# First mixer's last item spread over finer steps with full-row head weights and ScalarE copies; second mixer multiplies values and turns weights ahead of new scores

## Chip, cores and metric

One NeuronCore of one Trainium2 chip runs the whole program. The metric is the device time of one execution in microseconds (us), as the median of several runs. The program computes in float32; matmuls read float32r operands.

## What is computed

The input x is 512 tokens by 1024 features. Two blocks of two layers each follow one another. The change touches only the two attention mixers of the first block:

```python
def dilated_mixer(h, w_in, w_out):              # first mixer
    proj = (h @ w_in).reshape(B, S, 3 groups, 3, 16 heads, 64)
    for g, (window, dil) in enumerate(((128, 1), (512, 4), (2048, 16))):
        q, k = partial_rotary(proj[g, 0]), partial_rotary(proj[g, 1])
        o, lse = dilated_band_attention(q, k, proj[g, 2], dil, window // dil)
    wts = softmax(stack(lses), axis=groups)     # one weight per group, token, head
    o = einsum('gbsh,gbshd->bshd', wts, stack(outs))
    return o.reshape(B, S, 1024) @ w_out

def forgetting_mixer(h, w_in, b_f, w_out):      # second mixer
    q, k, v = h @ w_in;  c = cumsum(log_sigmoid(gates))
    s = q @ k^T / 8 + c_query - c_key, causal   # blocks of 128 queries
    return (softmax(s) @ v) @ w_out
```

After each mixer comes a SwiGLU layer, then a recurrent mixer and a retention mixer; these are unchanged.

## The kernel before

Activations lie feature by token. Every weight matrix is streamed in 353 units of 128 by 1024 through a ring of five slots. For each unit ScalarE rounds the weights into a high part WH (`split`, L1121) and VectorE computes the low part WL (L1711). TensorE multiplies in three passes, high by high, high by low and low by high, each a matmul with 512 columns. Instructions of each engine run in the order in which they are written; the order between engines is kept by semaphores.

The first mixer runs as six bodies (half of the heads by dilation group), each with 24 steps of 12 matmuls (L596 to L598 for queries and keys, L621 to L623 for values). Attention of the body before is strewn into the steps by a table written by hand: `place(phase, ticks, first, last)` spreads entries over the steps of a phase, phase 6 being the output projection (`AO`). An entry is one piece of attention for one item (a pair of heads): `scores` (L668, then mask and maximum on VectorE L1831, exponentials on ScalarE L1150), `turned` (the weights of head 0 or 1 transposed on TensorE L678 into bank 6, copied to A_PT by VectorE L1850 for head 0 and by ScalarE L1161 for head 1), `values` (L692, copied out to A_O by VectorE L1859), `weights` and `turn` (softmax over the three groups and its transposition, L701 and L707), `merge` (TensorE spreads one group's weights over the features of a tile, L715 and L716; VectorE multiplies A_O by it, L1883; GpSimd adds the groups, L1603 and L1607) and `low` (the high and low parts of the merged tile, L1171 and L1817). All engines walk through the same table.

The merge matmuls take 8 rows as operands: the weights of group g lie in rows 32g to 32g+7 of A_WH and A_WL, and A_SR holds a selection pattern in the same rows. Successive merges alternate between two banks of PSUM.

The output projection first works on feature tiles 0 to 3, four units of `pair_unit` with a step after every second of four row blocks (L596 to L598), then on tiles 4 to 7, four units with two steps each (L757 to L759), which read the A_YH and A_YL that `low` makes. R is the residual; VectorE adds the partial sums to it (L1939) after each of the first four units.

The second mixer has 88 steps of six matmuls and 32 items (a pair of heads by a block of 128 queries, so that an item has one to four blocks of keys). `forget_ticks` lists for item i the entries `norm` of i-1 (VectorE reciprocal L2047, GpSimd multiplication L1661), `scores` of i (L916; VectorE mask and maximum L2057 and L2059; ScalarE exponentials L1301), `values` of i-3 (L937; for the last block of a pair ScalarE makes B_OH, L1313, and VectorE B_OL, L2079) and `turned` of i-2, head 0; the next tick holds `turned` of head 1 (L926; copies L2076 on VectorE and L1309 on ScalarE). Both heads' transposes go to the same bank, so that those of head 1 wait for the copy of head 0. `place_b` gives each tick a step of its own, two or three steps per item, and two per item from step 66. These lines carry the order inside a step:

```python
                    (("norm", i - 1), 1 <= i <= B_ITEMS), (("scores", i), i < B_ITEMS),
...
                    (("values", i - 3), 3 <= i), (("turned", i - 2, 0), 2 <= i < B_ITEMS + 2)) if there])
...
                for entry in B_SPOT.get(g, ()):
                    forget(entry)
```

## Time and profile before

| | us |
|---|---|
| median of 3 runs | 2300.19 (2296.62 to 2302.95) |
| profiled execution, device time | 2301.07 |
| its span in the profile | 2299.3 |
| TensorE busy | 2227.8 |
| VectorE, ScalarE, GpSimd busy | 1203.8, 816.6, 492.5 |
| mean granted TensorE clock | 0.989 of full |

The span is that of the profiler; the execution's own time lies 1.8 us above it. A busy TensorE that is granted half its clock counts as busy, so the idle time and the clock are read apart. Matmuls of 512 columns last 0.39 us each and overlap, so that their spacing, not their length, is their cost.

### The profile page before, as it was taken

The page shows a single profiled execution, that of the slowest core. Times are in us where ns is not written, and L with a number is a line of the kernel's source. Part 1 is how long each engine was busy: PE and PEld are TensorE (multiplying, and loading weights), DVE is VectorE, ACT ScalarE, POOL GpSimd, SP SyncE. Part 2 cuts the span into 40 slices and gives each one's busy share as a digit, 9 for nine tenths or more (in the row PEclk, how much of TensorE's full clock was granted, in tenths as well). Part 3 has the DMA queues.
Part 4 walks back from the last instruction along what each step waited for, and adds up shares of the span by engine and source line. Part 5 has one row for each costly group of instructions (what it writes and reads, how often), then busy time and mean ns, then how long its engine had stood idle before and what let it go on. Part 6 is the DMA issues. An engine that isn't in the chain of part 4 may idle for free.

```text
span 2299.3 us, 26729 instructions
## 1 busy us (share of the span) xinstructions
PE 2227.8 (97%) x10598; PEld 1789.7 (78%) x10598; DVE 1203.8 (52%) x1995; ACT 816.6 (36%) x1360; POOL 492.5 (21%) x335
## 2 busy tenths in 40 slices
PE   8999999998999999999999999999998979999999
PEld 7788886887788888876667888888776857877877
DVE  4656556465654443355457444433788675443443
ACT  4434332434232222233433332322478323323322
POOL 2533234150511011123234110112111141100100
PEclk9999999999899999999999999999999999999999
DMA  4222221222233333332212333333332322222322
GB/s 154 83 65 83 74 83 56 65 77 62 67 98 94 99 98 95 101 102 74 92 56 83 93 100 95 98 101 93 92 94 81 100 69 83 87 78 75 96 71 85
DMA packets 85931, 198.27 MB, mean 86 GB/s; under 512 B 7328, under 2 KB 46496, under 8 KB 85808
## 3 DMA queue, kind: packets, MB, share of 16 engines
q1 hardware_dynamic: 83184, 189.62, 27.1%
q10 hardware_dynamic: 2624, 6.93, 0.9%
q8 instruction: 86, 1.41, 0.2%
q14 instruction: 37, 0.30, 0.1%
HBM read 194.40 MB, written 2.13 MB: 85 GB/s over the span
## 4 chain that ended last, share of the span: by engine, by line
PE 89%; DVE 5%; issue 2%; ACT 2%; POOL 1%; DMA 1%; SPq 0%; DVEq 0%; ACTq 0%; POOLq 0%
PE PS L550 52%; PE PS L596 6%; PE PS L598 5%; PE PS L597 5%; PE PS L621 2%; PE PS L623 2%; PE PS L622 2%; PE PS L1073 2%; PE PS L668 1%; PE PS L678 1%; PE PS L692 1%; PE PS L926 1%; PE PS L916 1%; PE PS L937 1%; PE PS L837 1%
## 5 line engine op out<-in xcount | busy, mean ns | idle before, releaser
L1711 DVE TENSOR_TENSOR WL<-WR,WH 128x1024 fp32r<-128x1024 f32 x353 | 468.2, 1332 | 732.8 <-ACT WH L1121 732.3
L1121 ACT ACTIVATE WH<-WR 128x1024 fp32r<-128x1024 f32 x353 | 371.1, 1056 | 692.0 <-DMA WR<-in_ws 680.9
L550 PE MATMUL PS<-XH,WH 128*128 128x512 f32 x1024 | 404.1, 395 | 18.9 <-ACT XH L1130 12.1
L550 PE MATMUL PS<-XL,WH 128*128 128x512 f32 x1024 | 400.5, 391 | 0.0
L550 PE MATMUL PS<-XH,WL 128*128 128x512 f32 x1024 | 400.5, 391 | 0.0
L550 PEld LDWEIGHTS PS<-XH,WH 128*128 128x128 f32 x1024 | 193.6, 189 | 63.4 <-issue 13.9
L550 PEld LDWEIGHTS PS<-XL,WH 128*128 128x128 f32 x1024 | 193.6, 189 | 41.4 <-issue 1.4
L550 PEld LDWEIGHTS PS<-XH,WL 128*128 128x128 f32 x1024 | 193.5, 189 | 40.5
L596 PE MATMUL PS<-XH,WH 128*128 128x512 f32 x544 | 224.8, 413 | 0.0
L598 PE MATMUL PS<-XH,WL 128*128 128x512 f32 x544 | 214.9, 395 | 0.0
L597 PE MATMUL PS<-XL,WH 128*128 128x512 f32 x544 | 214.3, 394 | 0.0
L1637 POOL TENSOR_TENSOR F_U<-F_G,F_U 128x1024 f32<-128x1024 f32 x22 | 52.6, 2392 | 399.5 <-DVE F_G L1977 399.5
L1615 POOL TENSOR_TENSOR A_SH<-A_SH,A_SIN 128x512 f32<-128x512 f32 x48 | 82.4, 1718 | 257.7 <-DVE A_SH L1897 257.7
L550 PE MATMUL PS<-HH,WH 128*128 128x512 f32 x352 | 136.9, 389 | 0.0
L550 PE MATMUL PS<-HL,WH 128*128 128x512 f32 x352 | 136.9, 389 | 0.0
L550 PE MATMUL PS<-HH,WL 128*128 128x512 f32 x352 | 136.9, 389 | 0.0
L1150 ACT ACTIVATE A_P<-A_P,A_ST 128x128 f32<-128x128 f32 (+1 forms) x192 | 79.7, 417 | 132.0 <-DVE A_ST L1840 132.0
L598 PEld LDWEIGHTS PS<-XH,WL 128*128 128x128 f32 x544 | 103.5, 190 | 23.4
L596 PEld LDWEIGHTS PS<-XH,WH 128*128 128x128 f32 x544 | 104.3, 192 | 21.9 <-issue 3.0
L597 PEld LDWEIGHTS PS<-XL,WH 128*128 128x128 f32 x544 | 104.2, 192 | 19.0
L550 PE MATMUL PS<-WH,XH 128*128 128x512 f32 x256 | 99.7, 389 | 0.0
L550 PE MATMUL PS<-WH,XL 128*128 128x512 f32 x256 | 99.6, 389 | 0.0
(327 smaller groups left out, 3715.9 us busy)
## 6 DMA issues: line engine op xcount, KB each, us to landing
WR<-in_ws SPq DMA_DIRECT2D x281, 512.0 KB, 3.6
WR<-in_ws SPq DMA_DIRECT2D x144, 256.0 KB, 3.2
B_CB<-gates ACTq DMA_DIRECT2D x8, 512.0 KB, 4.5
XTOK<-in_x SPq DMA_DIRECT2D x4, 512.0 KB, 5.9
out<-OUT SPq DMA_DIRECT2D x8, 256.0 KB, 2.0
R_D<-in_decay ACTq DMA_DIRECT2D x4, 256.0 KB, 2.6
GAIN<-in_post ACTq DMA_DIRECT2D x1, 512.0 KB, 4.8
CST<-in_cst SPq DMA_DIRECT2D x1, 256.0 KB, 6.5
```

The costliest lines, as they stand in the source:

```text
L550: mm = pe.matmul(PS[:, bank + o, :], l, r, start=first and kk == 0 and i == 0, stop=last and kk == 1 and i == 2)
L596: pe.matmul(PS[:, bank + o, :], WH[:, s, cols], hi[:, k, :], start=first, stop=False)
L597: pe.matmul(PS[:, bank + o, :], WH[:, s, cols], lo[:, k, :], start=False, stop=False)
L598: return pe.matmul(PS[:, bank + o, :], WL[:, s, cols], hi[:, k, :], start=False, stop=last)
L621: pe.matmul(PS[:, o, :], xh, wh, start=first and kk == 0, stop=False)
L622: pe.matmul(PS[:, o, :], xh, wl, start=False, stop=False)
L623: mm = pe.matmul(PS[:, o, :], xl, wh, start=False, stop=last and kk == 1)
L1121: nc.scalar.activation(WH[:, s, :], WR[:, s, :], ACT.Copy).then_inc(hi_ready, 1)
L1150: x = nc.scalar.activation(A_P[:, n % 2, h, w], A_P[:, n % 2, h, w], ACT.Exp, bias=stat(m, 0, 2 * pair + h, qb), accum_out=stat(m, 1, 2 * ...
L1615: nc.gpsimd.tensor_tensor(A_SH[:, r % 2, :], A_SH[:, r % 2, :], A_SIN[:, :], ALU.mult).then_inc(rot_m, 1)
L1637: nc.gpsimd.tensor_tensor(F_U[:, :, :], F_G[:, :, :], F_U[:, :, :], ALU.mult).then_inc(ht_ready, 1)
L1711: tt(WL[:, s, :], WR[:, s, :], WH[:, s, :].bitcast(F32), ALU.subtract).then_inc(lo_ready, 1)
```

## The change

1. **Output projection in finer steps.** In the first four units a step follows each row block (six matmuls): phase 6 has 24 steps instead of 16, numbers 0 to 15 of six matmuls and 16 to 23 of twelve.
2. **Last item table.** The entries of body 5 are placed by hand. The third item's scores come at step 22 of body 5 instead of step 0 of the projection; values come first in their steps; one or two merges stand in each of steps 8 to 14, the four `low` entries in steps 11, 13, 15 and 17.
3. **Copies.** Values of body 5 are copied to A_O by ScalarE instead of VectorE.
4. **Merges of the second half over 128 rows.** A new tile A_SEL (three patterns of 128 rows, made by three ScalarE copies at step 5 of the projection) takes the place of A_SR; A_WG, A_WH and A_WL become 128 rows, with zeros where no weights are. A_SEL lies over A_COS, A_SIN and A_SH.
5. **Second mixer.** Within a step the entries now stand as norm, values, turned, scores. VectorE sorts them as norm, turned, scores, values; ScalarE puts values first.

```diff
-        A_WG = a("A_WG", [P, TB, 96])
+        A_WG = a("A_WG", [P, TB, P])
...
-        late = scored(5)
...
-        place(5, late[:3], 18, 21)
-        place(6, late[3:], 0, 5)
-        place(6, [[("weights", 1)], [("turn", 1)]], 4, 5)
-        place(6, merged(1, (0, 1)) + [[("low", 0)]], 6, 7)
-        place(6, [[("low", 1)]] + merged(1, (2,)), 8, 8)
-        place(6, merged(1, (3,)) + [[("low", 2)]], 9, 9)
-        place(6, [[("low", 3)]], 10, 10)
+        place(5, [[last("scores", 0)], [last("scores", 1), last("turned", 0, 0)], [last("turned", 0, 1)]], 18, 21)
+        place(5, [[last("scores", 2)]], 22, 22)
+        place(6, [[last("values", 0), last("turned", 1, 0)], [last("turned", 1, 1), last("scores", 3)],
+                  [last("values", 1), last("turned", 2, 0)], [last("turned", 2, 1), ("weights", 1)],
+                  [last("values", 2), last("turned", 3, 0)], [last("turned", 3, 1)],
+                  [last("values", 3), ("turn", 1)], blended((0, 0), (0, 1)), blended((0, 2), (1, 0)),
+                  blended((1, 1), (1, 2)), blended((2, 0)) + [("low", 0)], blended((2, 1), (2, 2)),
+                  blended((3, 0)) + [("low", 1)], blended((3, 1), (3, 2)), [("low", 2)], [], [("low", 3)]], 1, 17)
...
-                    (("norm", i - 1), 1 <= i <= B_ITEMS), (("scores", i), i < B_ITEMS),
+                    (("norm", i - 1), 1 <= i <= B_ITEMS),
...
-                    (("values", i - 3), 3 <= i), (("turned", i - 2, 0), 2 <= i < B_ITEMS + 2)) if there])
+                    (("values", i - 3), 3 <= i), (("turned", i - 2, 0), 2 <= i < B_ITEMS + 2),
+                    (("scores", i), i < B_ITEMS)) if there])
...
+            return {"norm": 0, "turned": 1, "scores": 2, "values": 3}.get(entry[0], 4)
...
-                    pe.matmul(PS[:, bank, :], A_SR[rows, cols], A_WH[rows, :], start=True, stop=False)
-                    pe.matmul(PS[:, bank, :], A_SR[rows, cols], A_WL[rows, :], start=False, stop=True)\
+                    heads = A_SR[rows, cols] if half == 0 else A_SEL[:, g, cols]
+                    rows = slice(0, P) if half else rows
+                    pe.matmul(PS[:, bank, :], heads, A_WH[rows, :], start=True, stop=False)
+                    pe.matmul(PS[:, bank, :], heads, A_WL[rows, :], start=False, stop=True)\
...
+                elif ENTRIES[e][0] == "values" and ENTRIES[e][1] == 5:
...
+                    nc.scalar.activation(by_class(A_O[:, m % 4, pair, :], 2), classes_of(PS[:, O_BANK, :], 2), ACT.Copy)\
...
+                if i == 5:
+                    act.wait_ge(qk_ready, 48)
+                    for g in range(3):
+                        nc.scalar.activation(A_SEL[:, g, :].rearrange("p (h j) -> p h j", h=8),
...
-                for entry in B_SPOT.get(g, ()):
+                for entry in sorted(B_SPOT.get(g, ()), key=turned_first):
```

ScalarE at the passage from body 5 to the output projection, before (A_P and A_ST are the exponentials, A_V the copies of body 5's values out of PSUM):

```order
L1121 ACTIVATE WH<-WR 128x1024 [waits landed4]
L1230 ACTIVATE A_V<-PS,RB 128x512 [waits pv_done,rb_ready,v_half]
L1230 ACTIVATE A_V<-PS,RB 128x512
L1230 ACTIVATE A_V<-PS,RB 128x512 [waits unit_used]
L1230 ACTIVATE A_V<-PS,RB 128x512
L1121 ACTIVATE WH<-WR 128x1024 [waits landed0]
L1150 ACTIVATE A_P,A_ST<-A_P,A_ST 128x128 [waits nm_ready]
L1150 ACTIVATE A_P,A_ST<-A_P,A_ST 128x128 x3
L1150 ACTIVATE A_P,A_ST<-A_P,A_ST 128x128 [waits nm_ready]
L1150 ACTIVATE A_P,A_ST<-A_P,A_ST 128x128 x3
```

and now:

```order
L1138 ACTIVATE WH<-WR 128x1024 [waits landed4]
L1167 ACTIVATE A_P,A_ST<-A_P,A_ST 128x128 [waits nm_ready]
L1167 ACTIVATE A_P,A_ST<-A_P,A_ST 128x128 x3
L1167 ACTIVATE A_P,A_ST<-A_P,A_ST 128x128 [waits nm_ready]
L1167 ACTIVATE A_P,A_ST<-A_P,A_ST 128x128 x3
L1255 ACTIVATE A_V<-PS,RB 128x512 [waits pv_done,rb_ready,v_half]
L1255 ACTIVATE A_V<-PS,RB 128x512
L1255 ACTIVATE A_V<-PS,RB 128x512 [waits unit_used]
L1255 ACTIVATE A_V<-PS,RB 128x512
L1138 ACTIVATE WH<-WR 128x1024 [waits landed0]
L1185 ACTIVATE A_O<-PS 128x4x128 [waits y_sum,pv_done]
```

The exponentials of the third item have moved ahead of the four copies to A_V, and a copy to A_O stands ahead of the copy to A_PT.

TensorE at one item of the second mixer with three blocks of keys, before (B_K,B_Q are scores, B_PT,B_V values, CST,B_P transposes):

```order
L916 MATMUL PS<-B_K,B_Q 128x384 x2
L937 MATMUL PS<-B_PT,B_V 64x128 x8
L926 MATMUL PS<-CST,B_P 128x128
L596 MATMUL PS<-XH,WH 128x512
L597 MATMUL PS<-XL,WH 128x512
L598 MATMUL PS<-XH,WL 128x512
L596 MATMUL PS<-XH,WH 128x512
L597 MATMUL PS<-XL,WH 128x512
L598 MATMUL PS<-XH,WL 128x512
L926 MATMUL PS<-CST,B_P 128x128
```

and now:

```order
L954 MATMUL PS<-B_PT,B_V 64x128 x8
L943 MATMUL PS<-CST,B_P 128x128
L933 MATMUL PS<-B_K,B_Q 128x384 x2
L611 MATMUL PS<-XH,WH 128x512
L612 MATMUL PS<-XL,WH 128x512
L613 MATMUL PS<-XH,WL 128x512
L611 MATMUL PS<-XH,WH 128x512
L612 MATMUL PS<-XL,WH 128x512
L613 MATMUL PS<-XH,WL 128x512
L943 MATMUL PS<-CST,B_P 128x128
```

The scores have moved behind the values and the first transpose; the six matmuls of the step still lie between the two transposes.

VectorE at the same item, before (B_DG and B_CB are masks, B_OL the low part of a finished pair):

```order
L2057 ISA B_P,B_MX<-PS,B_CB 128x256
L2057 ISA B_MX 128x1
L2059 ISA B_P,B_MX<-PS,B_DG 128x128
L2059 ISA B_MX 128x1
L2068 TENSOR_SCALAR B_NM<-B_MX 128x1
L2057 ISA B_P,B_MX<-PS,B_CB 128x256
L2057 ISA B_MX 128x1
L2059 ISA B_P,B_MX<-PS,B_DG 128x128
L2059 ISA B_MX 128x1
L2068 TENSOR_SCALAR B_NM<-B_MX 128x1
L2079 TENSOR_TENSOR B_OL<-PS,B_OH 128x512
L2076 COPY B_PT<-PS 128x128
```

and now:

```order
L2078 RECIPROCAL B_RD<-B_DEN 128x2
L2107 COPY B_PT<-PS 128x128
L2088 ISA B_P,B_MX<-PS,B_CB 128x256
L2088 ISA B_MX 128x1
L2090 ISA B_P,B_MX<-PS,B_DG 128x128
L2090 ISA B_MX 128x1
L2099 TENSOR_SCALAR B_NM<-B_MX 128x1
L2088 ISA B_P,B_MX<-PS,B_CB 128x256
L2088 ISA B_MX 128x1
L2090 ISA B_P,B_MX<-PS,B_DG 128x128
L2090 ISA B_MX 128x1
L2099 TENSOR_SCALAR B_NM<-B_MX 128x1
```

The copy to B_PT, which was last, now comes ahead of masks and maxima, and B_OL follows them.

## Rows read from the trace of the kernel before

**Rows 1.** The page: busy us of each engine, share of the span, instructions.
```profile
PE 2227.8 (97%) x10598; PEld 1789.7 (78%) x10598; DVE 1203.8 (52%) x1995; ACT 816.6 (36%) x1360; POOL 492.5 (21%) x335
```

**Rows 2.** Windows: length, busy us of each engine, granted TensorE clock, DMA share, GB/s.
```profile
560.00:580.00 20.00, 16.28 (x58) 11.13 (x56) 12.20 (x16) 3.75 (x5) 5.35 (x4) 0.74 0.18 52
580.00:600.00 20.00, 16.54 (x60) 11.83 (x59) 8.98 (x10) 3.15 (x4) 5.37 (x4) 0.83 0.16 42
600.00:620.00 20.00, 20.00 (x90) 16.57 (x89) 17.21 (x18) 9.25 (x12) 14.74 (x11) 1.00 0.30 91
1015.00:1215.00 200.00, 187.30 (x1078) 131.62 (x1077) 101.62 (x395) 82.02 (x194) 62.96 (x79) 1.00 0.25 79
```

**Rows 3.** What TensorE waited for, 500 to 640 us: us, times, longest.
```profile
PE PS L757 <- DVE A_YL L1817: 4.7, 2, 2.8
PE PS L715 <- DVE A_O L1883: 2.5, 3, 0.9
PE PS L678 <- DVE A_PT L1850: 2.2, 1, 2.2
PE PS L701 <- issue: 0.9, 1, 0.9
```

**Rows 4.** TensorE timeline: start, length, line, operation, shapes, count, [idle before].
```profile
510.93 1.16 PE L668 MATMUL PS<-A_K,A_Q 64*128 64x128 f32 x16
...
563.38 0.50 PE L715 MATMUL PS<-A_WH,A_SR 8*128 8x512 f32 x2
563.72 0.40 PE L716 MATMUL PS<-A_WL,A_SR 8*128 8x512 f32 x2
...
574.34 0.77 PE L757 MATMUL PS<-A_YH,WH 128*128 128x512 f32 x1 [2.82 <-DVE A_YL L1817]
...
579.17 0.63 PE L759 MATMUL PS<-A_YH,WL 128*128 128x512 f32 x1
```

**Rows 5.** VectorE groups, 505 to 570 us: count, busy us, mean ns, idle before.
```profile
L1711 DVE TENSOR_TENSOR WL<-WR,WH 128x1024 fp32r<-128x1024 f32 x8 | 10.5, 1314 | 8.3 <-ACT WH L1121 8.3
L1859 DVE COPY A_O<-PS 128x512 f32<-128x512 f32 x4 | 4.3, 1068 | 3.0 <-PE PS L692 3.0
```

**Rows 6.** TensorE timeline: values of one item of the first mixer, transposes after them.
```profile
540.98 1.09 PE L692 MATMUL PS<-A_PT,A_V 128*64 128x128 f32 x16
542.01 0.66 PE L678 MATMUL PS<-CST,A_P 128*128 128x128 f32 x4
```

**Rows 7.** ScalarE timeline: exponentials of one item, copies of the values.
```profile
513.31 0.40 ACT L1150 ACTIVATE A_P<-A_P,A_ST 128x128 f32<-128x128 f32 x1 [6.80 <-DVE A_ST L1840]
...
516.32 0.19 ACT L1150 ACTIVATION_READ_ACCUMULATOR A_P<-A_P,A_ST 128x1 f32 x1
...
526.11 1.27 ACT L1230 ACTIVATE A_V<-PS,RB 128x512 f32<-128x512 f32 x2 [0.89 <-PE PS L623]
```

**Rows 8.** What TensorE waited for in the second mixer, 1015 to 1225 us.
```profile
PE PS L926 <- DVE B_PT L2076: 11.6, 12, 2.6
```

**Rows 9.** VectorE timeline around the longest of these waits.
```profile
1130.74 0.40 DVE L2057 CUSTOM_DVE_ANT_0 B_P<-PS,B_CB 128x256 f32<-128x256 f32 x1
...
1133.67 0.69 DVE L2079 TENSOR_TENSOR B_OL<-PS,B_OH 128x512 fp32r<-128x512 f32 x1 [1.26 <-ACT B_OH L1313]
1134.28 0.28 DVE L2076 COPY B_PT<-PS 128x128 f32<-128x128 f32 x1
```

**Rows 10.** TensorE timeline: scores of the item after it.
```profile
1136.34 1.13 PE L916 MATMUL PS<-B_K,B_Q 64*128 64x512 f32 x4
```

**Rows 11.** ScalarE timeline of that same item.
```profile
1139.51 0.73 ACT L1301 ACTIVATE B_P<-B_P,B_NM 128x512 f32<-128x512 f32 x1
...
1140.23 1.04 ACT L1121 ACTIVATE WH<-WR 128x1024 fp32r<-128x1024 f32 x1
```

**Rows 12.** A TensorE wait of 2.4 us elsewhere, and the window around its end.
```profile
1675.19 0.55 PE L1005 MATMUL PS<-CH,WH 128*128 128x512 f32 x1 [2.40 <-ACT L_R L1383]
...
1674.00:1678.00 4.00, 2.81 (x7) 2.27 (x8) 3.75 (x7) 3.99 (x7) 0.00 (x0) 0.69 0.09 36
```

More of the change, by code:

```diff
@@ L112, in program @@
         A_Y = a("A_Y", [P, 4, T])
+        A_SEL = sb("A_SEL", [P, 3, T], F32R, at=a.at)
         A_COS = a("A_COS", [P, T])
         A_SIN = a("A_SIN", [P, T])
+        A_SH = a("A_SH", [P, 2, T])
         A_P = a("A_P", [P, 2, 2, T])
         A_PT = a("A_PT", [P, 2, T])
-        A_SH = a("A_SH", [P, 2, T])
         A_MX = a("A_MX", [P, 2, 2, TB])
@@ L326, in program, with last, blended @@
         place(5, scored(4), 0, 14)
-        place(5, late[:3], 18, 21)
-        place(6, late[3:], 0, 5)
-        place(6, [[("weights", 1)], [("turn", 1)]], 4, 5)
-        place(6, merged(1, (0, 1)) + [[("low", 0)]], 6, 7)
-        place(6, [[("low", 1)]] + merged(1, (2,)), 8, 8)
-        place(6, merged(1, (3,)) + [[("low", 2)]], 9, 9)
-        place(6, [[("low", 3)]], 10, 10)
+        def last(kind, *rest):
+            return (kind, 5) + rest
+        def blended(*parts):
+            return [("merge", 1, t, j) for t, j in parts]
+        place(5, [[last("scores", 0)], [last("scores", 1), last("turned", 0, 0)], [last("turned", 0, 1)]], 18, 21)
[6 more added lines that the diff above has]
+                  blended((3, 0)) + [("low", 1)], blended((3, 1), (3, 2)), [("low", 2)], [], [("low", 3)]], 1, 17)
         for spot in sorted(SPOT):
@@ L411, in program, with turned_first, values_first @@
         place_b(forget_ticks(24, B_ITEMS + 3), 66, 86)
+        def turned_first(entry):
+            return {"norm": 0, "turned": 1, "scores": 2, "values": 3}.get(entry[0], 4)
+        def values_first(entry):
+            return 0 if entry[0] == "values" else 1
         B_TURNED = {7: [("q", 1, 0)], 8: [("q", 1, 1)], 15: [("k", 1, 0)], 16: [("k", 1, 1)],
@@ L735, in _ @@
                     pe.wait_ge(r_part, 2 * q - 2)
-                half_unit = pair_unit(U["AO"] + q, 0, XH, XL, 2 * (q % 2), True, True, x_ready(1))
-                for i in range(2):
+                half_unit = pair_unit(U["AO"] + q, 0, XH, XL, 2 * (q % 2), True, True, x_ready(1), every=1)
+                for i in range(4):
                     next(half_unit)
-                    for e in SPOT.get((6, 2 * q + i), ()):
+                    for e in SPOT.get((6, 4 * q + i), ()):
                         attend(e)
@@ L761, in _ @@
                             mm.then_inc(unit_used, 1)
-                    for e in SPOT.get((6, 8 + 2 * q + kk), ()):
+                    for e in SPOT.get((6, 16 + 2 * q + kk), ()):
                         attend(e)
@@ L1161, in attend @@
                     nc.scalar.activation(A_PT[:, 1, 0:w], PS[:, T_BANK, 0:w], ACT.Copy).then_inc(pt_copied, 1)
+                elif ENTRIES[e][0] == "values" and ENTRIES[e][1] == 5:
+                    _, m, i = ENTRIES[e]
+                    pair, segs, n = item(m, i)
+                    act.wait_ge(pv_done, n + 1)
+                    if pair == 0:
+                        act.wait_ge(y_sum, 8)
+                    nc.scalar.activation(by_class(A_O[:, m % 4, pair, :], 2), classes_of(PS[:, O_BANK, :], 2), ACT.Copy)\
+                        .then_inc(o_copied, 1)
                 elif ENTRIES[e][0] == "weights":
@@ L1232, in _ @@
             ao = U["AO"]
-            for i in range(16):
-                split(ao + i // 2 + 4)
+            for i in range(24):
+                split(ao + (i // 4 if i < 16 else i // 2 - 4) + 4)
+                if i == 5:
+                    act.wait_ge(qk_ready, 48)
+                    for g in range(3):
+                        nc.scalar.activation(A_SEL[:, g, :].rearrange("p (h j) -> p h j", h=8),
+                                             CST[:, IDENT + 32 * g:IDENT + 32 * g + 8].unsqueeze(2)
+                                             .to_broadcast([P, 8, HD]), ACT.Copy).then_inc(sel_ready, 1)
                 for e in SPOT.get((6, i), ()):
@@ L1318, in _ @@
                 split(bf + 9 + g // 4 + 4)
-                for entry in B_SPOT.get(g, ()):
+                for entry in sorted(B_SPOT.get(g, ()), key=values_first):
                     forget(entry)
@@ L1625, in _ @@
                         rotate(m, n)
-            for i in range(16):
+            for i in range(24):
                 for e in SPOT.get((6, i), ()):
@@ L1853, in attend @@
                     pair, segs, n = item(m, i)
-                    if closes(m, i):
+                    if closes(m, i) and m < 5:
                         g = A_BODIES[m][1]
@@ L1876, in attend @@
                     dve.wait_ge(st_hi, ENTRIES[e][1] + 1)
-                    tt(A_WL[0:96, :], PS[0:96, bank, :], A_WH[0:96, :].bitcast(F32), ALU.subtract)\
+                    tt(A_WL[:, :], PS[:, bank, :], A_WH[:, :].bitcast(F32), ALU.subtract)\
                         .then_inc(front_used, 1)
@@ L1930, in _ @@
             ao = U["AO"]
-            for i in range(16):
-                split(ao + i // 2 + 4)
+            for i in range(24):
+                split(ao + (i // 4 if i < 16 else i // 2 - 4) + 4)
                 for e in SPOT.get((6, i), ()):
                     attend(e)
-                if i % 2 and i < 8:
-                    q = i // 2
+                if i % 4 == 3 and i < 16:
+                    q = i // 4
                     dve.wait_ge(unit_used, ao + q + 1)
@@ L2083, in _ @@
                 split(bf + 9 + g // 4 + 4)
-                for entry in B_SPOT.get(g, ()):
+                for entry in sorted(B_SPOT.get(g, ()), key=turned_first):
                     forget(entry)
```

8 lines of the change are left out of this document (4 added, 4 removed).

## Prediction

> **What bounds the kernel now.** The page comes first. TensorE is busy for 2227.8 us, 97% of the span, the other engines for half of it or less [rows 1]. The program is one stream of matmuls, so a change can only win TensorE's idle time, the time in which it runs at less than its clock, or work of its own. The windows tell which of these lie near the change. In the output projection of the first mixer two windows of 20 us show TensorE busy for 16.3 and 16.5 us at a granted clock of 0.74 and 0.83, and the next one is full, 90 matmuls in 20 us [rows 2]: 0.22 to 0.23 us for a full matmul. The second mixer loses 12.7 us in 200 at full clock [rows 2]. The list of waits names the releasers. In the first place they are A_YL 4.7 us, A_O 2.5, A_PT 2.2 and 0.9 without one, 10.3 in all [rows 3]; in the second it is almost only VectorE's copy to B_PT, 12 waits and 11.6 us [rows 8].
>
> **The second mixer.** The longest of its waits shows the mechanism. The transposes of head 1 may not overwrite the bank before VectorE has copied head 0. VectorE does first the masks and maxima of the new item (from 1130.74), then B_OL, which waits 1.26 us for ScalarE's B_OH behind the exponentials, and only at 1134.28 the copy of 0.28 us [rows 9]. All of it belongs to scores that nobody needs yet. The change puts the copy ahead of the masks, and on TensorE the scores behind the first transposes. The copy (0.28 us here for one block; for four some 0.7, as B_OL takes 0.69 for a tile of that size from the same memory [rows 9]) can then start as soon as the transposes end, while TensorE has scores (up to 1.13 us [rows 10]) and six matmuls (1.4 us) ahead of the next transposes. Even with a WL of 1.3 us [rows 5] ahead of it the copy is in time. So all 11.6 us can go; what VectorE still does late is the B_OL, and the values of the next pair, which wait for it, stand two steps and more away.
>
> What is late next is ScalarE's copy of head 1, for which the values of the item wait. The exponentials stand ahead of it and now start later as TensorE sees it, because scores come last in the step. For an item with four key blocks scores end at 1136.34 + 1.13 = 1137.47 [rows 10] and the last exponential at 1139.51 + 0.73 + 0.18 = 1140.42 [rows 11]: 2.95 us, and 3.4 with the copy (some 0.4 us). TensorE meanwhile does two steps of six matmuls (2.8 us with the slower first matmul) and the transposes (0.3): 3.1 to 3.3 us where an item has two steps, which is so from step 66 on and for items 6, 12 and 18; 4.6 where it has three. So two items wait 0.1 to 0.3 us. A WH of 1.04 us between exponentials and copy [rows 11] gives 4.4 us; by the table this happens only where an item has three steps or few blocks. I take 0.6 us of new waits; the ends are 0, and 1.04 for each of the seven items that have a WH there, 7 us. The table speaks for the low end. The order of kinds on TensorE changes, their number does not; I cost that at nothing, and bound it by the 0.03 us that a first matmul could differ for 32 items, 1 us either way. Term: 11.6 - 0.6 = **11 us gained**.
>
> **The end of the first mixer, what goes.** Waits of 10.3 us [rows 3]. The clock: (1 - 0.74) x 20 + (1 - 0.83) x 20 = 8.6 us of full-speed time withheld [rows 2]; what falls on the 4.7 us of waits for A_YL costs nothing, half of them 2.4, so 6.2 us. The timeline agrees: between 574.34 and 579.17 twelve matmuls take 0.43 us each [rows 4], and there are 32 of these in four bursts. All bursts stand behind clusters of merges with 8 rows [rows 4], each with a wait. Sum 16.5 us. The change spreads the merges, one or two behind every six full matmuls, and gives them 128 rows. The waits for A_YL go, because each `low` now comes a step or more behind its merges and the projection reads it two to five steps later.
>
> **What comes.** Four things.
> First, the third item's scores now stand at step 22 of body 5, and on ScalarE their exponentials stand ahead of the four copies to A_V. Scores end at 512.09 and the first exponential starts at 513.31 [rows 4, 7]: 1.2 us. The sixteen parts of it last from there to 516.51, 3.2 us [rows 7], and two copies 1.27 [rows 7]: 5.7 us behind the scores. TensorE has twelve matmuls, 2.8 us, and then needs the banks: a **new wait of 2.9 us**, on the engine that everything waits for. Queued behind the copies on ScalarE is a WH whose unit TensorE needs three units on.
> Second, the group weights. They need the last item's exponentials, 4.4 us after its scores (1.2 + 3.2). In ScalarE's and VectorE's queues there then stand a copy to A_O (0.63 us as a copy to A_V [rows 7], or 1.07 as VectorE took for it [rows 5]), a WH of 1.04 [rows 11], a WL of 1.2 to 1.3 [rows 5] and the product A_MS (0.7, as a full tile): 8.0 to 8.5 us. TensorE has two chunks of six matmuls (2.8), values (1.05) and twice transposes (0.45 each) [rows 6]: 4.8. **New wait 3.3 us** (3.2 to 3.7).
> Third, the merges alternate between two banks, and VectorE must multiply each (0.68 us) between residual additions and WL. Before it cost 2.5 us [rows 3]; now six matmuls stand between pairs, but VectorE has 1.3 us of additions and 1.2 of WL at steps 7, 8, 11 and 12. Bounds 0 and 2.5; I take 1.5, since the pairs at steps 8, 9 and 13 meet this backlog.
> Fourth, the merges overlap no longer. The pair at 563.38 runs its four matmuls until 564.12, 0.74 us [rows 4]; at full rows they need 4 x 0.23 and a slower first, 0.95. Some five pairs: 1 us. Bounds 0 (the overlap may be modelled) and 1.5.
> The Trainium skill speaks against this part: "TensorE: Matmul & The Clock Gate", part 3 on packing small matmuls, says that matmuls with few rows in different row groups run concurrently, and that one of 32 rows takes as long as one of 128. By it each pair would go from the time of one merge to that of two, 2.5 to 3 us lost; the measured pair shows less than half of this overlap, so the row is used.
> Fifth, a price of these waits: the clock. A wait of 2.4 us elsewhere is followed by a window at 0.69, 1.2 us withheld [rows 12]; the wait of 2.2 us for A_PT [rows 3] is followed by none (the first reduced window is 560 to 580). The two new waits may cost 0 to 3 us together; I take 1.
> ScalarE's three copies to A_SEL (0.6 us each, as a copy to A_V [rows 7]) lie while it waits for the values of the third item: nothing; without that cover 1.8 us later A_O, still ahead of its use.
> Term: 16.5 - 2.9 - 3.3 - 1.5 - 1 - 1 = **6.8 us gained**, between 3 and 11.
>
> **Sum.** 11 + 6.8 = 17.8 us against the profiled execution's 2301.07: 2283.3, taken as **2283 us**. That execution lies 0.9 us above the median of 2300.19. Later stages are full of matmuls or wait for chains that start with TensorE's own end, so the gain is not taken back.
>
> **Rivals.**
> A. The clock stays low. The A_WH rows are zero but for 24 of 128, and the slow bursts may come from waits and not from rows: the burst at 574.34 begins right behind a wait of 2.8 us [rows 4]. Against: the first burst starts behind merges after a wait of only 0.9 [rows 3]. Then 5 of the 6.2 us stay: 2288. The same page, part 4, says that transposes do not count as work for the clock; by it the new wait at the weights, which stands behind transposes, would bring a burst (1.2 us). The row of the 2.2 us wait between transposes, at full clock, speaks against it.
> B. The new costs at the first mixer's end come at their upper ends, because ScalarE gets behind: A_V 4.5 us, weights 6, banks 2.5, clock 3, together 7.3 more than in the sum: 2291. For it: ScalarE gets four copies to A_O, three to A_SEL and the exponentials earlier than before. Against: it is idle for over half of this stretch.
> C. The second mixer's wait changes its place. The values wait for ScalarE's copy at half of the items by 0.4 us: 6 us given back, 2289.
> D. Slower. The same mechanism as C, with a point from which it decides: two-step items have 3.2 us and need 3.4, three-step items 4.6 and need up to 4.4. If masks and exponentials start one WL (1.2 us) later than I think, on all items, each waits about 0.8 us: 31 x 0.8 = 25 us, more than the 17.8 that is won, 2308. Against: VectorE is busy for half of the time.
> E. The change does not do what it says: masks queue on VectorE behind something else. The order of instructions shows the copy first at every item, so this needs the `norm` ahead of it to be late; by the 2.95 us above it is not. Part of C.
>
> **How the numbers follow.** Forecast (2278 to 2287) 0.60; A 0.12; B 0.11; C 0.11; B and C together or worse, at 2294 to 2299, 0.03; D 0.03. Below the forecast the bounds reach 2276 (no clock loss, no bank waits). The range 2276 to 2290 holds forecast, A and C and leaves out B, D and the worse, 0.17. 0.3%, about what can be told from no change, is 6.9 us, so faster is under 2293.3: forecast, A, B and C, 0.94; same 0.03; slower is D, 0.03.
>
> **What would show it.** In the windows 1015 to 1215 TensorE busy nearly throughout; in the waits no B_PT of more than 0.5 us in sum. At the projection's start a wait of some 2.9 us for A_V, then one of 3.3 us before the group weights, no wait for A_YL, windows at clock 1.00 but for one short burst, and TensorE's F0 matmuls 6 to 8 us earlier. It would be wrong if waits for ScalarE's B_PT copy show in the second mixer, or if merges over 128 rows run at 0.43 us a matmul.

## The result and the profile after

| | before | after |
|---|---|---|
| median, us | 2299.93 (4 runs) | 2285.64 (4 runs, 2284.32 to 2286.95) |
| profiled execution | 2301.07 | 2286.95 |
| its span | 2299.3 | 2285.1 |
| mean granted clock | 0.989 | 0.992 |

The ratio is 0.9938 [0.9921, 0.9955]: 14.3 us faster. The prediction was 2283 in a range from 2276 to 2290, "faster" with 0.94. The time is inside, 2.6 us above the centre. The gain does not come from the places in the shares that the sum gave them, and the experiments are about that. The lines and windows below are each of one profiled execution; a stretch of one stage can differ between two profiles of the same code, and the text says by how much where this bears on a reading.

**The second mixer.** What TensorE waited for, after, 1010 to 1230 us (us, times, longest):

```profile
PE PS L933 <- DVE B_MX L2090: 0.9, 1, 0.9
PE PS L954 <- ACT B_PT L1340: 0.4, 2, 0.2
```

The 11.6 us for VectorE's copy [rows 8] are gone, and ScalarE's copy is late twice by 0.2 us (the 0.9 us for B_MX stand in the profile before too). To see what that is worth, two landmarks are better than idle time: the first score (B_K, B_Q) and the first matmul on XH of the second feed-forward part. Tile statistics of TensorE, before (ns least/median/most, first and last start in us; the XH row of a stretch that ends at 1400):

```profile
L916 PE MATMUL PS<-B_K,B_Q x128: 272/482/694, 1021.5 to 1210.8; 64*128 64x128 f32 x32, 64*128 64x256 f32 x32, 64*128 64x384 f32 x32, 64*128 64x512 f32 x32
L550 PE MATMUL PS<-XH,WH x237: 387/389/799, 1238.1 to 1399.5; 128*128 128x512 f32 x119
```

and after:

```profile
L933 PE MATMUL PS<-B_K,B_Q x128: 272/481/693, 1019.0 to 1200.6; 64*128 64x128 f32 x32, 64*128 64x256 f32 x32, 64*128 64x384 f32 x32, 64*128 64x512 f32 x32
L565 PE MATMUL PS<-XH,WH x254: 387/389/799, 1227.0 to 1400.0; 128*128 128x512 f32 x127
```

1238.1 - 1021.5 = 216.6 us before, 1227.0 - 1019.0 = 208.0 after: 8.6 us gained, though 11.2 us of waits have gone. Part of the rest is in the order itself. TensorE's timeline of one item with three key blocks, before (start, length, line, operation, count):

```profile
1128.54 0.92 PE L916 MATMUL PS<-B_K,B_Q 64*128 64x384 f32 x4
1129.38 1.09 PE L937 MATMUL PS<-B_PT,B_V 128*64 128x128 f32 x16
1130.41 0.33 PE L926 MATMUL PS<-CST,B_P 128*128 128x128 f32 x1
1130.49 0.48 PE L596 MATMUL PS<-XH,WH 128*128 128x512 f32 x1
```

and after:

```profile
1124.19 1.09 PE L954 MATMUL PS<-B_PT,B_V 128*64 128x128 f32 x16
1125.22 0.33 PE L943 MATMUL PS<-CST,B_P 128*128 128x128 f32 x1
1125.47 0.92 PE L933 MATMUL PS<-B_K,B_Q 64*128 64x384 f32 x4
1126.32 0.50 PE L611 MATMUL PS<-XH,WH 128*128 128x512 f32 x1
```

From the first of these to the projection matmul, the same instructions take 1.95 us before and 2.13 after, and no wait is among them. The projection matmul starts 0.08 us after this transpose, the score only 0.25 us after it; all other steps are equal. (Where an item has several blocks, the last transpose is followed after 0.03 us by a projection matmul and after 0.20 by a score: the same difference.) Summed over the 29 stretches of this kind (from the last projection matmul ahead of one to the first behind it) it is 58.2 us before and 63.2 after, without the one wait of 0.2 us that falls into them: 5.0 us.

**The first mixer's end.** What TensorE waited for, after, 500 to 640 us:

```profile
PE PS L716 <- issue: 3.2, 1, 3.2
PE PS L611 <- ACT A_V L1255: 2.5, 1, 2.5
PE PS L732 <- DVE A_O L1914: 1.4, 2, 1.1
PE PS L774 <- DVE R L1970: 0.8, 1, 0.8
PE PS L636 <- DVE A_SH L1928: 0.6, 1, 0.6
PE PS L732 <- DVE A_WL L1908: 0.5, 1, 0.5
```

8.4 us without that for A_SH, which stood there before too, in place of 10.3 [rows 3]. L716 is the group weights, whose releaser the profile does not name ("issue"), L611 the projection's first matmul. The windows (columns as in [rows 2]):

```profile
520.00:540.00 20.00, 17.53 (x95) 15.46 (x94) 8.47 (x27) 13.43 (x39) 0.00 (x0) 0.91 0.17 54
540.00:560.00 20.00, 16.81 (x110) 13.61 (x109) 9.43 (x36) 9.45 (x26) 0.00 (x0) 0.83 0.08 27
560.00:580.00 20.00, 18.15 (x91) 13.56 (x90) 12.59 (x18) 5.27 (x7) 6.34 (x5) 1.00 0.17 52
580.00:600.00 20.00, 19.24 (x85) 15.56 (x84) 9.31 (x12) 5.40 (x6) 4.65 (x4) 1.00 0.26 80
```

From 560 to 600 us the clock is full, where it was 0.74 and 0.83 [rows 2]. It now falls earlier, behind both new waits, as the timeline shows:

```profile
533.88 0.80 PE L611 MATMUL PS<-XH,WH 128*128 128x512 f32 x1 [2.47 <-ACT A_V L1255]
534.47 0.63 PE L612 MATMUL PS<-XL,WH 128*128 128x512 f32 x1
...
536.94 0.39 PE L612 MATMUL PS<-XL,WH 128*128 128x512 f32 x1
...
550.99 3.65 PE L716 MATMUL PS<-A_MS,SPREAD 128*128 128x64 f32 x16 [3.19 <-issue]
554.39 0.77 PE L611 MATMUL PS<-XH,WH 128*128 128x512 f32 x1
554.97 0.63 PE L612 MATMUL PS<-XL,WH 128*128 128x512 f32 x1
```

A length of 0.63 us with starts 0.43 apart is the 1.2 GHz level, 0.39 and 0.23 the 2.4 GHz level. The landmark behind this stage is the first matmul of the first feed-forward part, 608.34 us before and 605.83 after:

```profile
608.34 0.39 PE L550 MATMUL PS<-XH,WH 128*128 128x512 f32 x1
```

```profile
605.83 0.39 PE L565 MATMUL PS<-XH,WH 128*128 128x512 f32 x1
```

The landmark ahead of it, where both kernels still have the same order, is the first score of body 5: at 510.93 before [rows 4], and after at

```profile
512.05 1.16 PE L683 MATMUL PS<-A_K,A_Q 64*128 64x128 f32 x16
```

So this stage took 97.4 us before and 93.8 after: 3.6 us gained, and 1.1 us of the profile after were lost ahead of it, in work that the change does not touch. Over all profiles here this score starts between 509.2 and 512.4 us.

3.6 + 8.6 = 12.2 us. The other 2 us of the 14.2 in the two spans are what the rest of the program gave: 1.1 lost ahead of the change, and 3.1 gained behind 1238 and 1227 us, where both kernels have the same instructions in the same order, 1061.2 us before and 1058.1 after. Over the profiles of all kernels here this part takes 1057.9 to 1062.4, for the most part because the same wait does or does not bring the clock down there. The wait of [rows 12] is in the profile after

```profile
1663.85 0.50 PE L1022 MATMUL PS<-CH,WH 128*128 128x512 f32 x1 [1.81 <-ACT L_R L1414]
1664.19 0.39 PE L1023 MATMUL PS<-CL,WH 128*128 128x512 f32 x1
```

and the clock stays up behind it.

### The profile page after: what moved, and what is told of

Read it like the earlier page. It is cut to its first block, busy times and chain, and to the rows that moved or that the text cites. A ratio compares the mean times of both kernels' runs of the same rounds, so it can differ in the third digit from the quotient of the medians.

```text
span 2285.1 us, 26732 instructions
## 1 busy us (share of the span) xinstructions
PE 2226.9 (97%) x10598; PEld 1790.5 (78%) x10598; DVE 1201.2 (53%) x1991; ACT 821.0 (36%) x1367; POOL 492.4 (22%) x335
## 3 DMA queue, kind: packets, MB, share of 16 engines
HBM read 194.40 MB, written 2.13 MB: 86 GB/s over the span
## 4 chain that ended last, share of the span: by engine, by line
PE 90%; DVE 5%; ACT 2%; issue 2%; POOL 1%; DMA 1%; SPq 0%; DVEq 0%; ACTq 0%; POOLq 0%
PE PS L565 52%; PE PS L611 6%; PE PS L613 5%; PE PS L612 5%; PE PS L636 2%; PE PS L637 2%; PE PS L638 2%; PE PS L1090 2%; PE PS L683 1%; PE PS L693 1%; PE PS L707 1%; PE PS L954 1%; PE PS L933 1%; PE PS L943 1%; PE PS L854 1%
## 5 line engine op out<-in xcount | busy, mean ns | idle before, releaser
L611 PE MATMUL PS<-XH,WH 128*128 128x512 f32 x544 | 226.0, 416 | 2.5 <-ACT A_V L1255 2.5
L611 PEld LDWEIGHTS PS<-XH,WH 128*128 128x128 f32 x544 | 104.5, 192 | 33.3 <-issue 10.1
```

The costliest lines, as they stand in the source:

```text
L611: pe.matmul(PS[:, bank + o, :], WH[:, s, cols], hi[:, k, :], start=first, stop=False)
```

## The experiments

Times are medians beside runs of the kernel before in the same session (2299.6 to 2300.9); the stage lengths come from one profile each. "Stage 1" is the time from the first score of body 5 to the first matmul of the first feed-forward part (97.4 us above), "stage 2" the time that was 216.6 us.

| first mixer's end | stage 1, us |
|---|---|
| as before (before, e1, e12, e9, e10) | 97.4, 97.5, 97.6, 99.2, 96.0 |
| before with 128-row merges (e8) | 92.7 |
| changed (after, e2) | 93.8, 92.7 |
| changed, with 8-row merges (e7) | 93.5 |
| changed with e3, e4, e5, e6 | 89.8, 86.6, 83.9, 82.5 |
| as e6 (e11) | 82.5 |

The five profiles of the same code in the first row differ by 3.2 us. Their waits are equal to 0.1 us; the granted clock is not: from 560 to 600 us it is 0.74 and 0.83 in three of them, 0.74 and 0.74 in e9, 0.86 and 0.80 in e10.

### e1: the second mixer's part alone

Edit: the kernel before, with the second mixer's table and both sorts of the change.

> The kernel before with the second mixer's new orders alone. Theory (the two halves are independent, and 11.2 us of the 14 come from here, since the waits for B_PT and B_MX fell from 12.5 to 1.3 us): 11 us faster than before, ratio 0.995, TensorE's wait for VectorE's B_PT copy at most 0.5 us in all, ScalarE's B_PT copy at most 1 us. Rival (part of the gain needs the earlier start of the layers between, or comes back later): less than 8 us.

Measured: 2291.64, ratio 0.9963 [0.9950, 0.9975], 9.3 us faster; stage 2 is 208.0 us, as in the whole change. It carries about 9 of the 14 us.

### e2: the first mixer's part alone

Edit: the change with the second mixer's table and sorts taken back.

> The changed kernel with the second mixer's orders as before. Theory: the first mixer's end alone gives 3 to 4 us (0.8 to 1.6 thousandths), because the two new waits of 2.5 and 3.2 us each bring a stretch at half clock; B_PT waits of 11 to 12 us stand as before. Rival (the second mixer's gain was smaller than its waits): 6 to 7 us as predicted.

Measured: 2296.74, ratio 0.9986 [0.9977, 0.9995], 4.2 us faster; the waits are those of after (3.2, 2.5, 1.4, 0.8, 0.5), the 11.6 us in the second mixer are back, and stage 1 is 92.7 us. The clock behind the wait for A_V stayed at its full level this time:

```profile
533.22 0.50 PE L610 MATMUL PS<-XH,WH 128*128 128x512 f32 x1 [2.47 <-ACT A_V L1254]
533.56 0.39 PE L611 MATMUL PS<-XL,WH 128*128 128x512 f32 x1
```

Same wait, same instructions around it, and stage 1 is 1.1 us shorter than after's. The two parts do not depend on each other as far as the times tell: 9.3 + 4.2 = 13.5 beside 14.3.

### e3: ScalarE copies the values first

```diff
-                    for e in SPOT.get((m, i), ()):
+                    for e in SPOT.get((m, i), ()) if m < 5 or i < 22 else ():
                         attend(e)
...
                                 .then_inc(v_ready, 1)
+                        for e in SPOT.get((m, i), ()) if m == 5 else ():
+                            attend(e)
```

> The changed kernel, but on ScalarE the copies to A_V stand ahead of the third item's exponentials at steps 22 and 23 of body 5. Theory (the wait for A_V and the half clock behind it are caused by the exponentials ahead of the copies): the wait of 2.5 us goes, the window 520 to 540 shows clock 1.00, and the kernel gains 2.5 + 1.2 = 3.7 us on the changed kernel, about 2282. Rival (the wait only moves on to the transposes or the weights, which need the same exponentials): the wait before the group weights grows by as much, gain under 1.5 us.

Measured: 2282.8, ratio 0.9927 [0.9913, 0.9940], 2.8 us less than the change. The wait for A_V is gone, the window 520 to 540 full, stage 1 89.8 us, 4.0 shorter than after's; the wait for the weights is still 3.2 us. The exponentials' 3.2 us ahead of the copies were the cause of the first wait, and moving them behind does not lengthen the second.

### e4: the projection's weight pieces two steps earlier

```diff
-                split(ao + (i // 4 if i < 16 else i // 2 - 4) + 4)
+                split(ao + ((i + 2) // 4 if i < 16 else i // 2 - 4) + 4)
```

on ScalarE and VectorE alike.

> The changed kernel, but in the output projection each WH and WL is made two steps earlier (steps 2, 6, 10, 14 instead of 4, 8, 12, 16). Theory (1.05 us of WH and 1.2 of WL stand between the last exponentials and the product A_MS): the wait before the group weights falls from 3.2 to about 1.0 us, the half clock behind it (weights 3.65 us instead of 1.5, six matmuls at 0.43) goes, gain 2.2 + 3 = 5 us, about 2281. Rival (the ring slot is not landed at step 2, so ScalarE waits for the transfer ahead of the exponentials): the wait stays at 3 us or grows.

Measured: 2280.19, ratio 0.9917 [0.9904, 0.9931], 5.5 us less than the change; stage 1 is 86.6 us, 7.2 shorter than after's (the part behind stage 2 took 1060.6 us and not 1058.1). The waits near the projection:

```profile
PE PS L611 <- ACT A_V L1255: 2.5, 1, 2.5
PE PS L774 <- DVE R L1970: 2.3, 1, 2.3
PE PS L716 <- issue: 0.8, 1, 0.8
```

The wait for the weights is 2.4 us shorter, as much as the WH of 1.04 and the WL of 1.3 us together [rows 5, 11] that stood ahead of A_MS, and the clock never leaves its full level. Behind the weights that follows the shorter wait; behind the wait for A_V, which is as long as in after, the clock stayed up as it did in e2 and e7, and that is not this edit's doing; it is worth 1.3 of the 7.2 us. A new wait comes up, for the residual additions. VectorE's timeline ahead of it:

```profile
573.93 1.46 DVE L1848 TENSOR_TENSOR A_YL<-A_Y,A_YH 128x512 fp32r<-128x512 f32 x1
575.31 1.27 DVE L1970 TENSOR_TENSOR R<-R,PS 128x512 f32<-128x512 f32 x2
```

TensorE waits for the second of these; the first, which is needed later, stands ahead of it.

### e5, e6: both together, and the additions first

e5 has the edits of e3 and e4. e6 besides turns the two around in step 15 of the projection:

```diff
-                for e in SPOT.get((6, i), ()):
+                for e in SPOT.get((6, i), ()) if i != 15 else ():
                     attend(e)
                 if i % 4 == 3 and i < 16:
...
+                for e in SPOT.get((6, i), ()) if i == 15 else ():
+                    attend(e)
```

> The changed kernel with the two edits of e3 (values copied by ScalarE ahead of the third item's exponentials) and e4 (the projection's weight pieces split two steps earlier on ScalarE and VectorE) together. Theory (each of the two waits costs its own length and the clock behind it, and the edits do not touch each other): neither the 2.5 us wait for the values nor the 3.2 us wait for the weights, clock 1.00 from 520 to 600 us; the new wait for the residual additions (2.3 us in e4) stays, because VectorE's order at that step is the same. e3 alone gave 2282.8, e4 alone 2280.2; together 2277.5, between 2276.5 and 2279. Rival (TensorE is ahead of VectorE behind the weights, so that each gain is taken back at the residual additions): that wait grows from 2.3 to about 4.8 us and the time is e4's, 2280.

Measured: 2277.01, ratio 0.9899 [0.9885, 0.9914]; stage 1 83.9 us. The two gains add up, as the theory said, and the wait for the additions stays at 2.3 us.

> e5 with one more edit: at step 15 of the projection VectorE makes the fourth pair of residual additions before the third low part of the merged heads (its addition stood behind a subtraction of 1.46 us in e4). Theory: the wait of 2.3 us for the residual additions goes or falls below 0.8 us, and the low part is needed only some steps later, so that nothing takes its place: 2 us faster than e5, 2275.5, between 2274 and 2277.5. Rival (the low part is needed as soon as it is ready): a wait of 1.5 to 2.5 us for it stands where that for the additions stood, and the time is e5's.

Measured: 2276.39, ratio 0.9900 [0.9885, 0.9915]. The wait for R, of e6:

```profile
PE PS L774 <- DVE R L1972: 0.9, 1, 0.9
```

Stage 1 is 82.5 us, 1.4 less than e5's, which is what the wait lost (2.3 to 0.9), and e11, with the same first mixer, has 82.5 again. The whole time shows 0.6 us, which can't be told from nothing.

### e7: the change with merges of 8 rows

```diff
-                    heads = A_SR[rows, cols] if half == 0 else A_SEL[:, g, cols]
-                    rows = slice(0, P) if half else rows
+                    heads = A_SR[rows, cols]
```

> The changed kernel, but the second half's merges take the heads' repetition from the 8-row table (A_SR) as the kernel before does, in place of the 128-row one; order, waits and copies stay. Theory 1 (it was the 8-row merges that kept the clock down from 560 to 600 us): granted clock below 0.9 in both windows from 560 to 600, time 3 to 6 us longer than the changed kernel's 2285.6, 2289 to 2291.5. Theory 2 (it was the waits among them that did, and the new order has none there): the clock stays at 1.00, a pair of merges takes about 0.75 us rather than 0.95, and the time is 2284.5 to 2286.

Measured: 2287.15, ratio 0.9946 [0.9929, 0.9963], not to be told from the change's 2285.64. The windows of e7 that had 0.74 and 0.83 before:

```profile
560.00:580.00 20.00, 18.06 (x87) 11.33 (x86) 13.16 (x19) 5.18 (x7) 6.65 (x6) 1.00 0.19 52
580.00:600.00 20.00, 18.98 (x84) 14.85 (x83) 8.91 (x11) 5.40 (x6) 4.29 (x3) 1.00 0.25 80
```

In the new order the clock stays up with 8 rows too. The merges' overlap is real and brings nothing: the first pair of merges takes 0.75 us from its start to the next matmul, with 128 rows 1.01, but from there to the end of stage 1 it is 41.1 us in e7 and 40.2 in after and e2. So the 8 rows cost 0.8 us rather than save 1. Waits for A_O and R that are together 0.3 us longer are part of that, and matmuls behind 8-row merges whose successors come later (0.34 us in e7, 0.24 in after). The Trainium skill says ("TensorE: Matmul & The Clock Gate", part 3) that matmuls with few rows in different row groups run at the same time; the first pair agrees in part, the stage shows no gain.

### e8: the kernel before with merges of 128 rows

Edit: in the kernel before, the two lines of e7 the other way round, A_SEL filled by ScalarE at step 4 of the projection, A_WG, A_WH and A_WL with 128 rows.

> The kernel before, but the second half's merges run over 128 rows (A_SEL, filled by ScalarE at step 4 of the projection); its order stays, so its waits of 10.3 us from 560 to 600 stay too. Theory 1 (rows set the clock): granted clock at least 0.95 from 560 to 600 us, against 0.74 and 0.83, and 3 to 6 us faster than before, 2295 to 2298. Theory 2 (waits set the clock): 0.74 to 0.85 there as before, and the time as before or up to 2 us longer (three copies of ScalarE of about 0.55 us each), 2300 to 2303.

Measured: 2297.34 (10 runs), ratio 0.9986 [0.9976, 0.9995]. Its windows, and rows of its timeline:

```profile
560.00:580.00 20.00, 16.66 (x76) 12.26 (x75) 13.82 (x21) 3.76 (x5) 5.40 (x4) 0.91 0.17 52
580.00:600.00 20.00, 17.78 (x70) 13.87 (x70) 8.87 (x10) 4.22 (x5) 5.40 (x4) 0.91 0.17 54
```

```profile
566.55 0.50 PE L718 MATMUL PS<-A_WH,A_SEL 128*128 128x512 f32 x1 [0.67 <-DVE A_O L1892]
...
567.72 0.39 PE L597 MATMUL PS<-XH,WH 128*128 128x512 f32 x1
...
573.92 0.47 PE L760 MATMUL PS<-A_YH,WH 128*128 128x512 f32 x1 [2.36 <-DVE A_YL L1826]
...
574.76 0.63 PE L760 MATMUL PS<-A_YH,WH 128*128 128x512 f32 x1
```

The kernel before, behind its merges:

```profile
566.34 0.80 PE L596 MATMUL PS<-XH,WH 128*128 128x512 f32 x1
566.93 0.63 PE L597 MATMUL PS<-XL,WH 128*128 128x512 f32 x1
```

Both theories are half right. With 8 rows the merges and a wait of 0.9 us among them were followed by matmuls at the 1.2 GHz level from 566.3 to 569.5; with 128 rows, and a wait of 0.67, they are not. A burst of this kind is there in all five profiles with the first mixer as before; for 128 rows in that order there is the one profile. Behind the longer wait for A_YL the clock falls in before (2.8 us) and in e8 (2.4), in e8 only after three matmuls. In e10 it does not:

```profile
572.60 0.47 PE L758 MATMUL PS<-A_YH,WH 128*128 128x512 f32 x1 [2.82 <-DVE A_YL L1818]
```

Twelve matmuls run there at the full level, and the burst comes behind the next merges, from 577.7 us. So neither rows nor waits alone say when the clock falls.

The rows alone give 2.9 us of time and a stage 1 of 92.7 us, where the whole first part of the change (e2) has 4.2 and 92.7. Not all of that is the clock: the waits for A_O fell from 2.5 to 1.3 us and those for A_YL from 4.7 to 4.3. e7's order alone gives the full clock from 560 to 600 us without the rows. The change has two remedies for one loss, and next to the rows its new order, with its two new waits, shows no gain that can be told from none; it gains once e3 and e4 take those waits away.

### e9, e10, e12: whose order is it in the second mixer

e9 has the kernel before with the two sorts only:

```diff
-                for entry in B_SPOT.get(g, ()):
+                for entry in sorted(B_SPOT.get(g, ()), key=turned_first):
```

(on ScalarE with `values_first`), so that TensorE keeps scores, values, turned heads.

> The kernel before with the second mixer's new order on VectorE (turned heads first) and ScalarE (values first) alone; TensorE keeps scores, values, turned heads. In the profiles of before, of the change and of e1 the 29 stretches in which TensorE does all three take 58.2 us with the old order and 63.2 us with the new one, 0.17 us each, though no wait stands in them. Theory 1 (VectorE's order takes the waits away, TensorE's costs 5 us and gives nothing): the wait of 11.6 us for VectorE's copy falls below 2 us, the time from the first score to the first matmul of the second feed-forward part goes from 216.6 to about 203.5 us (e1: 208.0), and the whole to 2287, between 2285 and 2290. Theory 2 (VectorE's copy, now first, waits for transposes that TensorE issues behind scores and values, and holds back the maxima behind it): a wait for the copy, the maxima or ScalarE's exponentials of 4 us or more stays, the stretch takes 208 to 216 us and the whole 2292 to 2300.

Measured: 2287.65, ratio 0.9946 [0.9933, 0.9958]; stage 2 from 1023.1 to 1226.8, 203.7 us. TensorE's waits in it:

```profile
PE PS L945 <- ACT B_PT L1317: 1.1, 2, 0.8
PE PS L924 <- DVE B_MX L2067: 0.9, 1, 0.9
PE PS L604 <- ACT B_V L1298: 0.7, 1, 0.7
```

Theory 1 holds: VectorE's order takes the waits away, and without TensorE's the 29 stretches take 58.1 us. This is 4.0 us less than e1, which differs from it in TensorE's order alone.

e10 has the change's table in the kernel before, without the sorts.

> The counterpart: the kernel before with the second mixer's new order on TensorE alone (turned heads, values, scores); VectorE still takes the scores' maxima ahead of the copy of turned heads. Theory 1: the copy stands behind maxima that wait for scores which now come last, so the wait for the copy stays at 11.6 us or grows, and the 5 us of the order come on top: first score to first matmul of the second feed-forward part 220 to 235 us, the whole 2303 to 2318. Theory 2 (TensorE's order is what removes the waits): 208 us and 2291.6 as in e1.

Measured: 2291.98, ratio 0.9961 [0.9946, 0.9976], as e1. The expectation was wrong, and for a plain reason: all engines read that table, so VectorE followed (values, turned heads, scores), and this was no test of TensorE's order. It shows that with the new table the sorts add nothing that the time shows (stage 2 is 209.0 us, in e1 208.0). e12 makes the test, with VectorE and ScalarE sorted back:

```diff
+            return {"norm": 0, "scores": 1, "values": 3, "turned": 4}.get(entry[0], 2)
...
-                for entry in B_SPOT.get(g, ()):
+                for entry in sorted(B_SPOT.get(g, ()), key=as_before):
```

> e10's edit changed the table that all engines read, so that VectorE and ScalarE followed it; here they are sorted back into the old order, and TensorE alone takes turned heads and values ahead of scores. Theory 1 (the copy comes in time only if VectorE takes it ahead of the maxima): with scores last on TensorE the maxima, and the copy behind them, come some 1.5 us later than before, so the wait for VectorE's copy is at least the 11.6 us of before and the 5.0 us of TensorE's order stay; first score to first matmul of the second feed-forward part 220 us or more (before 216.6), the whole 2303 to 2320. Theory 2 (either engine's order is enough, since TensorE's transposes stand earlier): the wait for the copy is below 2 us, 208 us and 2292 as in e1 and e10.

Measured: 2321.82, ratio 1.0092 [1.0075, 1.0109], 22 us slower than before. The wait for the copy in e12:

```profile
PE PS L931 <- DVE B_PT L2081: 23.4, 17, 2.5
```

and the window of its stage 2 (columns as in [rows 2]):

```profile
1021.20:1262.10 240.90, 216.64 (x1179) 148.38 (x1179) 112.45 (x410) 85.47 (x200) 64.30 (x81) 0.97 0.21 66
```

The wait doubles, and the clock falls to 0.97 over the stage (at most 7 us withheld), where it was full with 11.6 us of waits. The order that decides is VectorE's: TensorE's new order does harm without it and costs 5 us with it.

### e11: the best of it

e6 with TensorE's old order in the second mixer and VectorE's and ScalarE's new one.

> e6 (values copied first, weight pieces split early, residual additions first) with TensorE's old order in the second mixer, VectorE's and ScalarE's new one. Theory 1: 5 us faster than e6's 2276.4, 2271.5, between 2270 and 2274. Theory 2: as e6 or up to 8 us slower, 2276 to 2284.

Measured: 2272.44, ratio 0.9882 [0.9867, 0.9897]: 13.2 us faster than the change, 28 faster than before. Its waits are 0.9, 0.8, 0.6 and 0.5 us in the first mixer's end, and in the second mixer those of e9, 1.3 us (ScalarE's copy), 0.9 and 0.7; stage 2 is 203.8 us.

## Why the prediction was right, and where it was not

**Second mixer: 11 us forecast, 8.6 in the profile, 9.3 in e1.** The mechanism was right: the copy behind the maxima, and no other wait of size in its place (0.4 us, 0.6 forecast). Rivals C and D, values that wait for ScalarE's copy, did not come. The step that failed is "The order of kinds on TensorE changes, their number does not; I cost that at nothing, and bound it by [...] 1 us either way". It costs 5.0 us in the 29 stretches, and about 0.7 more since a projection matmul behind scores has its successor 0.34 us later, behind a transpose 0.31, at 30 places. In the other direction the waits were worth more than their idle time: the wait of 2.58 us stands for 2.97 from start to start where 0.23 would do, 2.74. Over the twelve waits that alone is some 2 us; e9 gives the whole of it, since there 9.8 us fewer of waits shorten stage 2 by 12.9 with TensorE's order unchanged: about 3 us. 11.6 + 3 - 0.4 - 5.7 is 8.5, against 8.6 measured. The two errors hid each other in part, and e9 shows what either was worth. With them known, the forecast should have said that the TensorE half of this edit loses time.

**First mixer's end: 6.8 us forecast, 3.6 in the profile, 4.2 in e2.** The waits came as worked out: for A_V 2.5 us (2.9 forecast), at the weights 3.2 (3.3). The banks took 2.7 with A_WL and R (1.5 forecast, upper end 2.5). The overlap of the merges, priced at 1 us, costs nothing to give up (e7). The term that was mis-sized is the clock's: "The two new waits may cost 0 to 3 us together; I take 1". In the profile it is 4.2 us. Behind A_V seven matmuls start within 3.06 us, in e7 within 1.72: 1.3 us. The sixteen weights take 3.40 us to the next matmul where e8's took 1.78, and the six matmuls behind them 2.84 instead of e4's 1.56: 2.9 us. 16.5 - 2.5 - 3.2 - 2.7 - 4.2 = 3.9 us, against 3.6 measured in the stage; in e2, whose clock did not fall behind A_V, 5.2 against 4.7. The prediction's sign "TensorE's F0 matmuls 6 to 8 us earlier" did not come: they start 2.5 us earlier, and still only 3.6 with the 1.1 us counted that this profile had lost ahead of the stage. Nor did "but one short burst": there are two.

**"The slow bursts" and rival A.** The forecast held both the order and the 128 rows for the cause of the clock's return. The clock did return from 560 to 600 us, so A, which had it stay low there, fell. But e7 and e8 say that each of the two is enough for the burst behind the first merges. The bursts behind the waits for A_YL stay in e8 and go in the new order, which has no such wait; that one such wait in e10 had none behind it shows that they are not certain either. The rule that A drew from the Trainium skill ("TensorE: Matmul & The Clock Gate", part 4: transposes do not count as work for the clock in the same way) would have brought a burst at the weights. There is one, in all four profiles with that wait of 3.2 us (after, e2, e3, e7). These waits are longer than the 2.2 us for A_PT, which also stands between transposes and is followed by none, so the runs do not say whether the transposes or the length decide.

**The sum.** 17.8 us forecast, 14.3 measured. By the landmarks of the two profiles the change gave 12.2, and the 2 us more of these profiles come from work that it does not touch; that part is luck. e1 and e2 give 13.5 by their times. Each half came out below its centre and within its own bounds, so that the time is inside the range for the right reasons, with the clock's and the order's prices wrong. B had the right place (clock 3, banks 2.5) at too high a price for A_V and the weights.

## What to carry to other kernels

When a wait names a copy that stands behind other work on its engine, reorder that engine and leave TensorE's order alone until a run says that it matters; test each engine's order by itself, since one table may move them all. Price a reordering of matmuls by the start-to-start times of each pair of neighbours, which the timeline shows, not by the count of instructions. Judge small edits by two landmarks in the timeline, one ahead of the place and one behind it: their distance showed 1.4 us (e6, and e11 again), where the whole time, with its 4.5 us of play behind, could not. One landmark is not enough, since the start of the stage itself moves by 3 us from profile to profile. And compare the clock inside the stage before a difference of 3 us is put down to the edit: the same code had 96.0 to 99.2 us. When a change has several parts, run each alone: the 128 rows by themselves gave about as much as the whole new first part.

## What the runs showed of the hardware that was not expected

- A single transpose followed by a score (64 rows) costs 0.25 us from start to start, followed by a projection matmul 0.08. A score or a value matmul behind a projection matmul starts 0.32 to 0.33 us after it, another projection matmul 0.23 and a transpose 0.23. Values behind scores show no such step. Why is open.
- The same wait of 2.5 us, in the same surroundings, was followed by a lower clock in one of four profiles (after; not e2, e4, e7) and one of 3.2 us in all four that have it (after, e2, e3, e7). The Trainium skill ("TensorE: Matmul & The Clock Gate", part 1) says that the chip's activity window runs free, so that the number of slow matmuls varies from run to run. This fits, but would fit other outcomes too.
- 23.4 us of waits of up to 2.5 us in the second mixer brought the clock to 0.97 there (e12), 11.6 us of waits of up to 2.6 left it at 1.00 in before and e2, and brought one burst in e8 (0.99, stage 2 217.9 us), whose second mixer is the same.
- ScalarE's copy out of PSUM into A_O, which puts the tokens apart by dilation class, took 1.09 us, against 0.67 for one to A_V of the same size in plain order (after).
